# Inverting the 16x16 diagonal blocks of both prompt delta rules as two 8x8 blocks at once and a corner by two products

## The reference

```
M = jnp.where(strict, jnp.einsum('nbhid,nbhjd->nbhij', kb, kc) * gamma, 0.0)
Tinv = lax.linalg.triangular_solve(eye + M, eye, left_side=True, lower=True)
u = Tinv @ (vc * bc[..., None])
wk = Tinv @ (kb * jnp.exp(G)[..., None])
def step(S, inp):
    v_new = ui - wi @ S
    o = (qi * jnp.exp(Gi)[..., None]) @ S + Ai @ v_new
    S = S * jnp.exp(Gl)[..., None] + jnp.einsum('bhcd,bhce->bhde', ki * jnp.exp(Gl - Gi)[..., None], v_new)
```

## Time and profile before

| what | us |
|---|---|
| three runs: median (lowest, highest) | 4412.67 (4377.76, 4418.99) |
| profiled execution: span from first to last instruction | 4393.3 |
| busy in the span: TensorE, VectorE, GpSimd, ScalarE | 3858.2, 2228.7, 1229.2, 940.1 |

### The profile page before, as it was taken

How to read it: one execution, slowest core, us unless ns; L and a number is a source line. 1 busy time by engine, 2 the same in 40 slices (tenths; PEclk the granted TensorE clock), 3 DMA queues, 4 the chain that set the end, 5 groups by cost and what they waited for, 6 DMA issues and landing times. The chain is left out here.

```text
span 4393.3 us, 64529 instructions
## 1 busy us (share of the span) xinstructions
PE 3858.2 (88%) x23932; PEld 3576.1 (81%) x23932; DVE 2228.7 (51%) x4008; ACT 940.1 (21%) x1746; POOL 1229.2 (28%) x930
## 2 busy tenths in 40 slices
PE   8997688857989889999999799867886889999997
PEld 8997477746753489999999699766785879999996
DVE  3254688433220226655556566327764166565654
ACT  2000333125332211111111222113442021111112
POOL 4221233222000123323332133214443243333331
PEclk9999788767689899999999899887886989999998
DMA  5244211022026211111110122222214121111111
GB/s 176 82 154 165 64 54 26 5 85 72 1 86 205 77 38 53 50 36 53 33 53 24 32 94 92 84 72 64 73 37 106 38 58 34 54 37 53 33 43 49
DMA packets 365848, 290.63 MB, mean 66 GB/s; under 512 B 100831, under 2 KB 326175, under 8 KB 365333
## 3 DMA queue, kind: packets, MB, share of 16 engines
q1 hardware_dynamic: 317624, 231.15, 18.1%
q10 hardware_dynamic: 48060, 57.33, 3.8%
HBM read 216.39 MB, written 73.99 MB: 66 GB/s over the span
## 5 line engine op out<-in xcount | busy, mean ns | idle before, releaser
L982 PE MATMUL fup_acc<-ffn_high,fup_wh 128*128 128x364 f32 (+1 forms) x2112 | 699.8, 331 | 46.8 <-POOL fup_wl L906 42.5
L983 PE MATMUL fup_acc<-ffn_low,fup_wh 128*128 128x364 f32 (+1 forms) x2112 | 698.5, 331 | 0.0
L984 PE MATMUL fup_acc<-ffn_high,fup_wl 128*128 128x364 f32 (+1 forms) x2112 | 696.1, 330 | 0.0
L982 PEld LDWEIGHTS fup_acc<-ffn_high,fup_wh 128*128 128x128 f32 x2112 | 400.4, 190 | 48.9 <-POOL fup_wl L906 41.3
L1163 DVE TENSOR_TENSOR trunk_xT<-fup_dn,trunk_xT 128x364 f32<-128x364 f32 x528 | 282.7, 535 | 255.1 <-PE fup_dn L1014 255.1
L983 PEld LDWEIGHTS fup_acc<-ffn_low,fup_wh 128*128 128x128 f32 x2112 | 400.8, 190 | 0.0
L984 PEld LDWEIGHTS fup_acc<-ffn_high,fup_wl 128*128 128x128 f32 x2112 | 400.5, 190 | 0.0
L1012 PE MATMUL fup_dn<-fup_gh,fup_dh 128*128 128x364 f32 (+1 forms) x1056 | 346.9, 328 | 0.0
L1013 PE MATMUL fup_dn<-fup_gl,fup_dh 128*128 128x364 f32 (+1 forms) x1056 | 345.9, 328 | 0.0
L1014 PE MATMUL fup_dn<-fup_gh,fup_dl 128*128 128x364 f32 (+1 forms) x1056 | 345.4, 327 | 0.0
L335 PE MATMUL p_acc<-p_wh,even_in_high 128*128 128x296 f32 (+1 forms) x936 | 281.4, 301 | 10.5 <-DVE even_in_low L374 7.9
(11 more groups left out here) (718 smaller groups left out, 8459.2 us busy)
## 6 DMA issues: line engine op xcount, KB each, us to landing
fup_ws<-in_ffn_w_up SPq DMA_DIRECT2D x88, 512.0 KB, 3.9
fup_ds<-in_ffn_w_down SPq DMA_DIRECT2D x22, 1024.0 KB, 5.9
fs_kp<-in_cache_fox_k SPq DMA_DIRECT2D x64, 256.0 KB, 2.9
fs_vp<-in_cache_fox_v SPq DMA_DIRECT2D x64, 256.0 KB
ev<-p_o ACTq DMA_DIRECT2D x104, 148.0 KB, 1.8
p_ws<-in_ev_w_in SPq DMA_DIRECT2D x12, 1184.0 KB, 6.9
qkv<-gqkv_conv ACTq DMA_DIRECT2D x24, 544.0 KB, 2.7
gqkv_ws<-in_od_w_in SPq DMA_DIRECT2D x24, 512.0 KB, 4.1
```

What stands on the lines that cost most here:

```text
L982: pe.matmul(ps, wh[:, b, k], xh[:, k, c0:c0 + w_], start=(k == 0), stop=False)
L983: pe.matmul(ps, wh[:, b, k], xl[:, k, c0:c0 + w_], start=False, stop=False)
L984: mm = pe.matmul(ps, wl[:, b, k], xh[:, k, c0:c0 + w_], start=False, stop=(k == KD - 1))
```

## The change

The 16x16 block is held in a tile of 272 elements a partition, of which the first 256 are the square; a second view, `diagonal_blocks`, takes its two 8x8 diagonal blocks as one pattern (136 elements apart). `invert_blocks` inverts both at once, in seven rounds of a multiply and a sum. The lower left corner then comes from two matrix products, each cut into two pieces of 4 rows or columns so that known zeros are left out: `left_product` and `right_product` in RWKV, `join_blocks` in GDN. Between them one 8x8 block is copied to its transpose. In every multiply the summed index is contiguous in both operands. For that RWKV works column by column from the right and uses the transposed matrix that its `subN` holds, and GDN keeps the transpose `subXT` as the working tile and copies `subX` from it at the end, into the tile of `subN`. In the slots `substitute` is replaced in place: `invert_blocks` stands where the first part stood, the products where the later parts stood. GpSimd's two memsets set up `subXT` instead of `subX` in GDN. The DMAs are the same in number and size.

```diff
--- before.py
+++ after.py
@@ -1797,6 +1797,21 @@
     if len(ap.shape) == 2:
         return ap.rearrange("p (a q w) -> p a q w", q=2, w=w)[:, :, second, :]
     return ap.rearrange("p h (a q w) -> p h a q w", q=2, w=w)[:, :, :, second, :]
+
+
+Q8 = 8
+DIAGONAL = 2 * Q8 * (2 * Q8 + 1)
+
+
+def square(flat):
+
+    return flat[:, :4 * Q8 * Q8].rearrange("p (r c) -> p r c", c=2 * Q8)
+
+
+def diagonal_blocks(flat):
+
+    both = flat.rearrange("p (b x) -> p b x", b=2)[:, :, :2 * Q8 * Q8]
+    return both.rearrange("p b (r c) -> p b r c", c=2 * Q8)[:, :, :, :Q8]
 
 
 def rwkv_weights(ph):
@@ -2272,7 +2287,9 @@
         y, gw, bv = (ph.sb(n, [P, RW_W]) for n in ("y", "gw", "bv"))
         u0, u = ph.sb("u0", [P, RW_W]), ph.sb("u", [P, RW_W])
         S0 = ph.sb("S0", [P, PR, P])
-        subN, subX, subXT, subP = (ph.sb(n, [NBLK * H, BASE, BASE]) for n in ("subN", "subX", "subXT", "subP"))
+        flatN, flatX = (ph.sb(n, [NBLK * H, DIAGONAL]) for n in ("subN", "subX"))
+        subN, subX = square(flatN), square(flatX)
+        subXT, subP = (ph.sb(n, [NBLK * H, BASE, BASE]) for n in ("subXT", "subP"))
         zero = ph.sb("zero", [P, 2])
         lowT = ph.sb("lowT", [P, 2, P])
         cen, strict = (ph.sb(n, [P, P]) for n in ("cen", "strict"))
@@ -2888,19 +2905,39 @@
                 dve.wait_ge(s["rk_done"], i + 1)
                 dve.tensor_reduce(bon[:, i], heads(rk[:]), AX.X, ALU.add).then_inc(s["bon_done"], 1)
 
-            def substitute(i, first, last):
-
-                if first == 1:
-                    dve.wait_ge(s["setup"], 3)
-                    dve.wait_ge(s["sub_in"], 16 * (i + 1))
-                    if i:
-                        dve.wait_ge(s["x_out"], 32 * i)
-                for r in range(first, last):
-                    step(dve.tensor_tensor(subP[:, :r, :r], bc(subN[:, :r, r], 1, r),
-                                           subX[:, :r, :r].rearrange("p j c -> p c j"), ALU.mult))
-                    step(dve.tensor_reduce(subX[:, r, :r], subP[:, :r, :r], AX.X, ALU.add))
-                if last == BASE:
-                    dve.tensor_copy(subXT[:], subX.rearrange("p r c -> p c r")).then_inc(s["sub_done"], 1)
+            def invert_blocks(i):
+
+                dve.wait_ge(s["setup"], 3)
+                dve.wait_ge(s["sub_in"], 16 * (i + 1))
+                if i:
+                    dve.wait_ge(s["x_out"], 32 * i)
+                for c in range(Q8 - 2, -1, -1):
+                    n = Q8 - 1 - c
+                    prod = subP.rearrange("p a b -> p (a b)")[:, :2 * n * n].rearrange("p (b r j) -> p b r j", b=2, r=n)
+                    step(dve.tensor_tensor(prod, diagonal_blocks(flatX)[:, :, c + 1:, c + 1:],
+                                           bc(diagonal_blocks(flatN)[:, :, c, c + 1:], 2, n), ALU.mult))
+                    step(dve.tensor_reduce(diagonal_blocks(flatX)[:, :, c + 1:, c], prod, AX.X, ALU.add))
+
+            def product(out, a, b):
+
+                rows, cols, n = out.shape[1], out.shape[2], a.shape[2]
+                prod = subP.rearrange("p a b -> p (a b)")[:, :rows * cols * n]\
+                    .rearrange("p (r c j) -> p r c j", r=rows, c=cols)
+                step(dve.tensor_tensor(prod, bc(a, 2, cols), bc(b, 1, rows), ALU.mult))
+                step(dve.tensor_reduce(out, prod, AX.X, ALU.add))
+
+            def left_product():
+
+                for r0, js in ((4, slice(Q8, BASE)), (0, slice(Q8, Q8 + 4))):
+                    rows = slice(Q8 + r0, Q8 + r0 + 4)
+                    product(subX[:, rows, :Q8], subX[:, rows, js], subN[:, :Q8, js])
+
+            def right_product():
+
+                step(dve.tensor_copy(subXT[:, :Q8, :Q8], subX[:, :Q8, :Q8].rearrange("p r c -> p c r")))
+                for c0 in (0, 4):
+                    product(subX[:, Q8:, c0:c0 + 4], subX[:, Q8:, c0:Q8], subXT[:, c0:c0 + 4, c0:Q8])
+                dve.tensor_copy(subXT[:], subX.rearrange("p r c -> p c r")).then_inc(s["sub_done"], 1)
 
             def add_join(i, q):
                 for g in range(2):
@@ -2972,7 +3009,7 @@
                 if new:
                     add_rkv(t + 2)
                 if nxt:
-                    substitute(t + 1, 1, 7)
+                    invert_blocks(t + 1)
                 if new:
                     sum_k(t + 2)
                 if now:
@@ -2980,12 +3017,12 @@
                 if new:
                     add_rank(t + 2)
                 if nxt:
-                    substitute(t + 1, 7, 10)
+                    left_product()
                 if new:
                     decays(t + 2)
                     keys(t + 2)
                 if nxt:
-                    substitute(t + 1, 10, BASE)
+                    right_product()
                 if now:
                     add_join(t, 1)
                 if old:
@@ -3132,8 +3169,9 @@
         NL = [[ph.sb(f"NL{q}{g}", [P, HF, P]) for g in range(2)] for q in range(2)]
         PX = [ph.sb(f"PX{g}", [P, HF, P]) for g in range(2)]
         w, y, S = (ph.sb(n, [P, H, DK]) for n in ("w", "y", "S"))
-        subN, subX, subP = (ph.sb(n, [ROWS, BASE, BASE]) for n in ("subN", "subX", "subP"))
-        subXT = subP
+        flatN, flatXT = (ph.sb(n, [ROWS, DIAGONAL]) for n in ("subN", "subXT"))
+        subN, subXT = square(flatN), square(flatXT)
+        subX, subP = subN, ph.sb("subP", [ROWS, BASE, BASE])
         Xc, XcT = (ph.sb(n, [P, H, BASE]) for n in ("Xc", "XcT"))
         junk = ph.sb("junk", [P, HF, P], mybir.dt.bfloat16)
         diag = ph.sb("diag", [P, 2, P], mybir.dt.bfloat16)
@@ -3537,9 +3575,9 @@
 
         @block.gpsimd
         def _(pool):
-            pool.memset(subX[:], 0.0).then_inc(s["zeroed"], 1)
+            pool.memset(subXT[:], 0.0).then_inc(s["zeroed"], 1)
             pool.wait_ge(s["zeroed"], 1)
-            pool.memset(subX.rearrange("p r c -> p (r c)")[:, 0:BASE * BASE:BASE + 1], 1.0).then_inc(s["zeroed"], 1)
+            pool.memset(subXT.rearrange("p c r -> p (c r)")[:, 0:BASE * BASE:BASE + 1], 1.0).then_inc(s["zeroed"], 1)
             pool.memset(S[:], 0.0).then_inc(s["zeroed"], 1)
 
             def level(i, q):
@@ -3619,19 +3657,35 @@
         def _(dve):
             step = Chain(dve, s["dve_step"])
 
-            def substitute(i, first, last):
-
-                if first == 1:
-                    dve.wait_ge(s["zeroed"], 2)
-                    dve.wait_ge(s["sub_in"], 16 * (i + 1))
-                    if i:
-                        dve.wait_ge(s["x_out"], 32 * i)
-                for r in range(first, last):
-                    step(dve.tensor_tensor(subP[:, :r, :r], bc(subN[:, r, :r], 1, r),
-                                           subX[:, :r, :r].rearrange("p j c -> p c j"), ALU.mult))
-                    step(dve.tensor_reduce(subX[:, r, :r], subP[:, :r, :r], AX.X, ALU.add))
-                if last == BASE:
-                    dve.tensor_copy(subXT[:], subX.rearrange("p r c -> p c r")).then_inc(s["sub_done"], 1)
+            def invert_blocks(i):
+
+                dve.wait_ge(s["zeroed"], 2)
+                dve.wait_ge(s["sub_in"], 16 * (i + 1))
+                if i:
+                    dve.wait_ge(s["x_out"], 32 * i)
+                for r in range(1, Q8):
+                    prod = subP.rearrange("p a b -> p (a b)")[:, :2 * r * r].rearrange("p (b c j) -> p b c j", b=2, c=r)
+                    step(dve.tensor_tensor(prod, diagonal_blocks(flatXT)[:, :, :r, :r],
+                                           bc(diagonal_blocks(flatN)[:, :, r, :r], 2, r), ALU.mult))
+                    step(dve.tensor_reduce(diagonal_blocks(flatXT)[:, :, :r, r], prod, AX.X, ALU.add))
+
+            def product(out, a, b):
+
+                rows, cols, n = out.shape[1], out.shape[2], a.shape[2]
+                prod = subP.rearrange("p a b -> p (a b)")[:, :rows * cols * n]\
+                    .rearrange("p (r c j) -> p r c j", r=rows, c=cols)
+                step(dve.tensor_tensor(prod, bc(a, 2, cols), bc(b, 1, rows), ALU.mult))
+                step(dve.tensor_reduce(out, prod, AX.X, ALU.add))
+
+            def join_blocks():
+
+                for c0 in (0, 4):
+                    product(subXT[:, c0:c0 + 4, Q8:], subXT[:, c0:c0 + 4, c0:Q8], subN[:, Q8:, c0:Q8])
+                step(dve.tensor_copy(subX[:, Q8:, Q8:], subXT[:, Q8:, Q8:].rearrange("p c r -> p r c")))
+                for r0, js in ((4, slice(Q8, BASE)), (0, slice(Q8, Q8 + 4))):
+                    rows = slice(Q8 + r0, Q8 + r0 + 4)
+                    product(subXT[:, :Q8, rows], subXT[:, :Q8, js], subX[:, rows, js])
+                dve.tensor_copy(subX[:], subXT.rearrange("p c r -> p r c")).then_inc(s["sub_done"], 1)
 
             def add_join(i, q):
                 for g in range(2):
@@ -3730,11 +3784,11 @@
                 if has(t - 2):
                     scale_y(t - 2)
                 if nxt:
-                    substitute(t + 1, 1, 6)
+                    invert_blocks(t + 1)
                 if now:
                     add_join(t, 0)
```

(2 more changed lines are left out.)

## The result

| | us |
|---|---|
| after, 19 runs: median (lowest, highest) | 4365.47 (4319.25, 4391.18) |
| before, 19 runs on the same chip: median (lowest, highest) | 4410.44 (4366.0, 4428.83) |
| after as a share of before | 0.9905, 95% interval 0.9875 to 0.9934 |
| span of the profiled execution after | 4381.1 |
| VectorE busy in it | 2179.6 |

The change makes the kernel 0.95% faster, 42 us of 4410 (29 to 55 by the interval). The two profiled spans differ by 12.2 us only. That is no contradiction: by the offsets at which the same stages start in both traces, the untouched FoX prompt stage, which lies between the two, took 25 us longer in the execution profiled after, the GDN stage 38.9 us less, the RWKV stage 0.3 more. In the thirteen profiles of this document that untouched stretch takes from 392 to 425 us, whatever the kernel. So the stages are compared here, not the spans.

A forecast was written before the change was run, and what follows sets the result against it. In GDN it took TensorE's waits on VectorE, the clock behind them and a circuit through the DMAs as the bound, in RWKV both engines level; -32.3 (GDN slots) - 2.4 (first block) - 1 (RWKV) gave 4377 us, range 4350 to 4415.

The forecast's parts named there:

- The prices: VectorE instruction costs in both stages: inversion and products 6.8 us against 9.2, so 2.4 us less, eight times a stage.
- the rival that the short rows cost 1.80 ns: VectorE multiplies in both stages stay at the strided rate: 4380 us; chance included in the forecast's 0.60.
- The GDN slot: GDN: wait of `grams` for `values` gone, slot 35.3 us; six slots 211.8 instead of 244.1, 32.3 us less.
- the first block: GDN's first block stands alone on VectorE and gives its 2.4 us.
- only the waits come back: GDN: clock stays at 1.2 GHz through `join(t,1)`, so waits alone give 15.9 us; 4393 us, chance 0.20.
- More: GDN: no GpSimd hold-up, 2.4 GHz kept after the first pause, slot 31.7 us; 4353 us, chance 0.10.
- Slower: GDN: undivided inversion lengthens the first pause, half clock through `join(t,1)`, slot 42.3 us; 4428 us, chance 0.10.
- RWKV: RWKV stage: first two blocks -2.3 us each, later slots +3.6 together; -1 us, bounds -6 and +8.
- TensorE's 16.2 us from L2404 to `join(t,1)`: RWKV: TensorE's time from third low-rank product to `join(t,1)` unchanged, starting 0.7 us later.
- The sum: Whole kernel: -32.3 - 2.4 - 1 = -35.7 us from a median of 4412.67, giving 4377 us.
- the held-up copy: GDN's last copy waiting for GpSimd: VectorE's part 5.4 us, still under TensorE's 7.55, so `values` never late.

The follow-up runs named there:

- e11: Changed kernel, GDN only: `add_join` first, `values` ahead of the products, GpSimd made to wait until the products are done; ratio to before 0.9835.
- e1: Kernel before with the new inversion in RWKV alone, GDN keeping the old one; ratio to before 1.0005.
- e5: Kernel before, GDN only: old fifteen rounds in their old places on the transposed tile, summed index contiguous, no 8x8 blocks; ratio to before 0.9965.
- e3: Changed kernel with each multiply of GDN's products done three times, result unchanged; one run, 4395.02 us (before 4418.06).
- e4: Changed kernel with each multiply of GDN's products done five times, result unchanged; one run, 4490.43 us (before 4421.67).
- e9: Kernel before, GDN only: old fifteen rounds with contiguous summed index, `values` moved ahead of the last copy; one run, 4367.57 us (before 4421.67).
- e10: Changed kernel, RWKV only: `add_join(t,0)`, `add_rank` and `decays` ahead of the inversion, both products after the keys; ratio to before 0.9859.
- e6: Changed kernel, GDN only: `add_join(t,0)` ahead of `invert_blocks`, `values` ahead of `join_blocks`; ratio to before 0.9925.
- e7: Changed kernel, RWKV only: `add_join(t,0)` and `add_rank` ahead of key sum and inversion, `left_product` while TensorE cumulates; ratio to before 0.9917.

## Why the prediction was right

- *The prices.* Foretold: 0.15 us and 1.04 ns an element for contiguous multiplies. That gives 0.42 us for 256 products; 0.41 was measured. `invert_blocks` was to take 3.1 us, and takes 3.11 where GpSimd is away (3092.19 to 3095.30 in e11). The products were to take 3.7, and take 3.65. So the rival that the short rows cost 1.80 ns is out.
- *The GDN slot.* Foretold 35.3, measured 35.9 in the slot shown. By its own terms: block start to `add_join`, 3.1 + 1.0 foretold and 3120.40 to 3124.62 = 4.22 measured; then to L3342, 0.8 and 0.79; L3342 to L3322, 7.55 and 7.14; L3322 to the last `mask_grams`, 15.24 and 16.39; the DMAs, 7.6 and 7.40. The terms hold one by one in this slot, not only in the sum; over the six slots L3342 to L3322 runs from 4.81 to 7.34, so that 7.55 was its upper end. Six slots give -31.2 against -32.3, the first block 28.77 - 26.66 = 2.1 against 2.4.
- *The clock.* The rival "only the waits come back" wanted `join(t,1)` to stay at 0.50; it has 1.00. "More" wanted the first pause to leave the clock alone; it did so in one slot of the six (3.81 us, 1.00), and in the others the clock falls to 0.50 behind it. "Slower" wanted the low clock of the first pause to last through `join(t,1)`; it is over before `grams`, as the short slot of the earlier trace rows had it. (The 9.6 us that "slower" read from the earlier trace rows hold the 3.29 us of waiting for `values`, which its own account does without.)
- *RWKV.* Foretold -1 us within -6 and +8; the stage moved by +0.3 in the profile, and e1 gives a ratio of 1.0005. The first two blocks gave 2.3 and 3.2 (foretold 2.3 each), the slots behind them gave 5.0 back (foretold 3.6). The pause ahead of the third low-rank product grew as foretold, 2.75 to 4.17 us before and 3.47 to 4.70 after in the last five slots, 0.8 on the mean, and VectorE waits 4 us a slot at `add_join(t,1)`. One step is wrong: that TensorE's 16.2 us from L2404 to `join(t,1)` would stay as they were. They were those of the only slot at full clock. That slot fell to 0.50 like the others, and grew from 45.45 to 48.94 us, 3.5 of the 5.0; that the sum came out near the forecast all the same is luck in part.
- *The sum.* -35.7 foretold. By the same terms the profiles give -31.2 - 2.1 - 0.5 = -33.8 (RWKV's stage by its block starts); by the offsets of the whole stages -38.6, of which 5.6 us lie in GDN ahead of the start of its first block and behind that of its last, where the prediction had 0; the runs give -42 (-55 to -29). 4377 against 4365.47, 12 us off; 2.2 of these come from the median of before, 4410.44 over 19 runs where I had 4412.67 from three, and the rest lies inside the interval.

What the prediction had not seen is how narrow the margin was. It named the held-up copy as a bound (5.4 us instead of 4.2 ahead of `values`, against 7.55) and took the wait for gone in either case. e5, e3 and e4 show that the held-up copy is a state of its own: once VectorE is so late that GpSimd's state scaling has begun, the multiplies and copies left are held up, `values` slips further, and in most of these slots the half clock follows. The change gains because it ends before that point, more than because of the 2.4 us as such: e9 gets most of the gain without the 8x8 blocks. And for RWKV the prediction took the 16.2 us of one slot for all; the others paid 3.3 us more for the half clock behind a pause which the order of VectorE's list made, and e10, which takes the pause away, has the 16.2 us in each slot.

## What to carry to other kernels

Where a slow engine's work stands ahead of what TensorE waits for, look at the granted clock behind the wait before you shorten the work: putting the awaited instructions first brought 30 us in RWKV's stage, where a faster inversion had brought none. When a two-input VectorE operation takes two or three times its length, look which GpSimd instruction ran beside it; an engine with idle time can be made to wait, and in GDN that alone was worth 23 us of six slots (e6 to e11). And after moving an instruction, look for the next one in the list that the same engine waits for: the first try in RWKV only moved the pause.

## What the runs showed of the hardware

- Multiplies with one operand 16 elements apart cost 1.70 to 1.79 ns an element before (0.53 us for 225 in five blocks, 0.55 in the row that the prediction read), contiguous ones 1.02 to 1.03 (0.38 for 225, 0.41 for 256). The copies that transpose the same tile also read 16 elements apart, and took 0.37 us for 256 elements, less than a contiguous two-input multiply of that size (0.41); the sums that write single elements 16 apart cost nothing extra either (0.38 for 225, as before). The Trainium skill ("SBUF — State Buffer", Door 1: The DMA port swizzle) has lines of 16 bytes that full bandwidth wants hit more than once; the slower multiply agrees, the copy doesn't show it.
- A pause of TensorE can cost more than its length. Behind pauses of 3.44 us (after, L3342), 2.95 (e5) and 2.19 (e7) stand stretches at 0.50; in e4 some 12 us of it behind 11.63. Behind 0.74 us (e6, ahead of the first gram) it stayed at 1.00. The length alone does not decide: behind 2.75 us the clock stayed at 1.00 in one RWKV slot before and fell to 0.50 in another, and behind 3.81 us it stayed at 1.00 in one GDN slot after. No run here shows what does.
- A 0.37 us copy that came 0.14 us after the start of a GpSimd instruction of 1.90 us was held up until about its end, and took 1.98 us (e5).
